# A hybrid transformer block on one core: output projection divided along its contraction, gate units moved, post norms on VectorE, exponentials ahead of the next normalisation

## What is computed

```python
def token_mixer(x, ...):        # block 1: a state space branch and an mLSTM branch
    h = rmsnorm(x, g_pre); proj = h @ w_in
    ...
    return x + rmsnorm(merged @ w_out, g_post)          # post norm 1

def channel_mixer(x, ...):
    h = rmsnorm(x, g_pre)
    a = causal_dwconv(h @ w_gate, w_conv, b_conv)
    y = (gelu(a) * (h @ w_up)) @ w_down
    return x + rmsnorm(y, g_post)                       # post norm 3

def mixer_sublayer(x, ...):     # block 2
    proj = rms_norm(x, norm_g) @ w_in                   # q, k, v, 6 forget logits, gate of 384
    q = rms_norm(q, q_gain); k = rms_norm(k, k_gain)    # per head of 64, 16 heads
    # heads 0..3 MoBA (ALiBi), 4..9 forgetting attention, 10..15 dilated attention
    y_moba = rms_norm(o_moba, out_gain[:256])
    y_fox = rms_norm(o_fox, out_gain[256:640]) * sigmoid(g_fox)
    y_dil = rms_norm(o_dil, out_gain[640:])
    return x + concatenate([y_moba, y_fox, y_dil]) @ w_out

def mlp_sublayer(x, ...):
    return x + square(relu(rms_norm(x, norm_g) @ w_up)) @ w_down
```

## Time and profile before

| | us |
|---|---|
| median of 3 timed runs | 1643.73 |
| the profiled execution's own time | 1639.23 |
| its span, first to last instruction | 1637.4 |
| TensorE busy in the span | 1510.2 |
| VectorE busy | 861.7 |
| ScalarE (ACT) busy | 669.9 |
| GpSimd (POOL) busy | 301.8 |
| mean granted TensorE clock | 0.963 |

### The profile page before, as it was taken

One profiled execution on the slowest core, in us unless ns is written; L12 is line 12 of the kernel. 1 busy time (PEld: TensorE's weight loads), 2 busy tenths in 40 slices (PEclk: granted clock), 3 DMA queues, 4 the chain that ended last, 5 costly groups with the idle time before them and its releaser, 6 DMA issues.

```text
span 1637.4 us, 22270 instructions
## 1 busy us (share of the span) xinstructions
PE 1510.2 (92%) x8565; PEld 1304.7 (80%) x8565; DVE 861.7 (53%) x1252; ACT 669.9 (41%) x1042; POOL 301.8 (18%) x280
## 2 busy tenths in 40 slices
PE   6677689999997999999998798999879999999998
PEld 6677689999996988998886576888768788888887
DVE  4877824445737453454353736677753533434344
ACT  6656685554233222222123333645462522323140
POOL 0872310000013550461262200000010000000000
PEclk9788789999998999999999899999989999999999
DMA  5111112223321333233233121111113232323331
GB/s 188 46 52 43 36 52 65 65 65 110 111 91 31 99 90 103 81 96 97 86 91 115 52 77 40 52 34 46 39 39 100 67 103 90 99 89 96 90 101 64
DMA packets 35489, 126.63 MB, mean 77 GB/s; under 512 B 4396, under 2 KB 4524, under 8 KB 35280
## 3 DMA queue, kind: packets, MB, share of 16 engines
q1 hardware_dynamic: 33888, 120.61, 24.2%
q10 hardware_dynamic: 864, 4.33, 0.7%
q0 software_dynamic: 656, 0.56, 0.1%
HBM read 123.37 MB, written 2.10 MB: 77 GB/s over the span
## 4 chain that ended last, share of the span: by engine, by line
PE 79%; DVE 10%; ACT 7%; issue 2%; POOL 2%; DMA 0%; DVEq 0%; SPq 0%; ACTq 0%; POOLq 0%
PE ps L1541 67%; PE ps L1561 2%; DVE rot L765 2%; PE ps L1840 2%; PE ps L1866 2%; ACT u L395 2%; ACT y_a L501 1%; PE ps L1690 1%; PE ps L1853 1%; ACT w_hi L324 1%; PE ps L1821 1%; DVE w_lo L762 1%; PE ps L1641 1%; POOL acc L1413 1%; POOL conv_tmp L1499 1%
## 5 line engine op out<-in xcount | busy, mean ns | idle before, releaser
L1541 PE MATMUL ps<-h_hi,w_hi 128*128 128x264 f32 (+1 forms) x1792 | 529.6, 345 | 47.0 <-DVE h_lo L774 24.8
L1541 PE MATMUL ps<-h_lo,w_hi 128*128 128x264 f32 (+1 forms) x1792 | 508.8, 333 | 0.0
L1541 PE MATMUL ps<-h_hi,w_lo 128*128 128x264 f32 (+1 forms) x1792 | 507.3, 332 | 0.0
L762 DVE TENSOR_TENSOR w_lo<-w_raw,w_hi 128x1024 fp32r<-128x1024 f32 x223 | 290.7, 1304 | 213.9 <-ACT w_hi L324 212.6
L1541 PEld LDWEIGHTS ps<-h_hi,w_hi 128*128 128x128 f32 x1792 | 310.7, 192 | 96.6 <-issue 36.0
L1541 PEld LDWEIGHTS ps<-h_lo,w_hi 128*128 128x128 f32 x1792 | 307.0, 192 | 36.4 <-issue 7.7
L1541 PEld LDWEIGHTS ps<-h_hi,w_lo 128*128 128x128 f32 x1792 | 306.6, 192 | 31.2
L324 ACT ACTIVATE w_hi<-w_raw 128x1024 fp32r<-128x1024 f32 x223 | 232.7, 1051 | 223.0 <-PE ps L1541 222.0
L1541 PE MATMUL ps<-mlp_lo,w_hi 128*128 128x512 f32 x256 | 100.9, 394 | 0.0
L1541 PE MATMUL ps<-mlp_hi,w_hi 128*128 128x512 f32 x256 | 100.4, 392 | 0.0
L1541 PE MATMUL ps<-mlp_hi,w_lo 128*128 128x512 f32 x256 | 99.4, 388 | 0.0
(11 more groups left out here) (278 smaller groups left out, 2005.7 us busy)
## 6 DMA issues: line engine op xcount, KB each, us to landing
w_raw<-w_units SPq DMA_DIRECT2D x223, 512.0 KB, 3.6
x<-x_t ACTq DMA_DIRECT2D x1, 2112.0 KB, 8.1
out<-out_tile SPq DMA_DIRECT2D x8, 256.0 KB, 2.0
x<-x_t ACTq DMA_DIRECT2D x3, 528.0 KB, 9.3
x<-x_t ACTq DMA_DIRECT2D x2, 264.0 KB, 4.6
b_raw<-ssm_b SPq DMA_DIRECT2D x1, 512.0 KB, 11.0
c_raw<-ssm_c SPq DMA_DIRECT2D x1, 512.0 KB, 12.3
dil<-dil POOLq DMA_DIRECT2D x1, 512.0 KB, 3.8
```

The costliest lines, as they stand in the source:

```text
L762: Dv.do(v.tensor_tensor(wlo[:, s % RING, :], raw[:, s % RING, :], f32(whi[:, s % RING, :]), ALU.subtract), lo_ready)
L1541: ins = mm(o, wt[:, s % RING, w], xt[:, kx, c0:c0 + n], start=(b == 0 and a == 0), stop=(b == len(blocks) - 1 and a == 2))
```

## The change

1. **Post norms.** POOL's six multiplications go; VectorE multiplies all eight tiles, each before its addition to `x`, with `h_lo` of the tile before in between.
2. **Gate units.** Gate unit 0 runs before q unit 0, gate units 1 and 2 after k unit 0. Their sigmoids run in front of iteration 1. The loop over pairs is now i = 1 .. 7.
3. **Exponentials ahead.** ACT does `exps(i-1,1)` before `qk_rsqrt(i,1)`, VectorE `weigh(i-1,1)` before `qk_norm(i,1)`. The squares of groups 0 and 1 move to iterations 5 and 6.
4. **Projection.** Its contraction is divided: eight units of five blocks (tiles 0 to 4, MoBA and gated heads; 15 matmuls each) and four units that hold the last three blocks of two output tiles each (18 matmuls). Tiles 0 to 4 are transposed, gated and split within iteration 7, into PSUM banks of the q and k units. The eight parts stand between the steps of the last three heads. The last four units write banks 2, 3, 6 and 7, from `y_dil_hi` and `y_dil_lo`. Splits of these units take 640 or 768 columns.
5. **Start of the MLP.** x, h4 and its squares follow pair by pair behind the last four units; squares have a buffer each (`mlp_sq`).

```diff
+KA, KB = 5, 3
+OB_BANK = (2, 6)
-U_QK2 = U_F2 + 1
-U_GFOX = U_QK2 + 2 * KT
-U_OUT2 = U_GFOX + 3
-U_MLP = U_OUT2 + KT
+U_G0 = U_F2 + 1
+U_QK2 = U_G0 + 1
+U_OA = U_QK2 + 2 * KT + 2
+U_OB = U_OA + KT
+U_MLP = U_OB + KT // 2
...
 ACT
+            qk_square(0, 0)
+            split_hi(qk_unit(0, 0) + LOOK)
+            qk_square(0, 1)
+            split_hi(qk_unit(0, 1) + LOOK)
+            qk_rsqrt(0, 0)
+            qk_rsqrt(0, 1)
+            split_hi(gate_unit(1) + LOOK)
+            split_hi(gate_unit(2) + LOOK)
+            for j in range(3):
+                act.wait_ge(evacuated, gate_unit(j) + 1)
+                A.do(dn.activation(sgf[:, j, :], sgf[:, j, :], ACT.Sigmoid), sem("sgf_ready"))
+            for i in range(1, KT):
+                last = i == KT - 1
+                if last:
+                    moba_gain(0)
                 if i >= 2:
                     pt_copy(i - 2, 1)
+                qk_square(i, 0)
+                if last:
+                    moba_gain(1)
+                exps(i - 1, 0)
+                split_hi(qk_unit(i, 0) + LOOK)
+                if i == KT - 3:
                     group_squares(0)
+                if i == KT - 2:
                     group_squares(1)
+                qk_rsqrt(i, 0)
+                if i == KT - 2:
                     group_rsqrt(2, 0, 2)
+                if not last:
+                    split_hi(qk_unit(i, 1) + LOOK)
+                qk_square(i, 1)
+                if last:
+                    y_hi(0)
+                    y_hi(1)
+                pt_copy(i - 1, 0)
+                if last:
+                    y_hi(2)
+                    y_hi(3)
+                    y_hi(4)
+                exps(i - 1, 1)
+                if last:
+                    split_hi(U_OA + 1)
+                qk_rsqrt(i, 1)
...
 VectorE
-                        if m < OWN_SCALED:
-                            tt(ysum[:, m, 0:n], ysum[:, m, 0:n], rs[:, 0:n], M)
-                            Dv.fence()
-                        else:
-                            dve.wait_ge(sem("y_scaled"), (KT - OWN_SCALED) * POST.index(norm) + m - OWN_SCALED + 1)
-                        stt(x[:, m, c0:T1], ysum[:, m, 0:n], col(gain, m), x[:, m, c0:T1], M, A_, sem(ready))
+                        tt(ysum[:, m, 0:n], ysum[:, m, 0:n], rs[:, 0:n], M)
                     if m:
                         dve.wait_ge(sem(hi), m)
                         stt(hlo[:, m - 1, 0:n], x[:, m - 1, c0:T1], col(pre, m - 1), f32(hhi[:, m - 1, 0:n]), M, S_, sem(lo))
+                    if m < KT:
+                        Dv.fence()
+                        stt(x[:, m, c0:T1], ysum[:, m, 0:n], col(gain, m), x[:, m, c0:T1], M, A_, sem(ready))
...
+            gate_evac(0)
+            qk_evac(0, 0)
+            split_lo(qk_unit(0, 0) + LOOK)
+            qk_evac(0, 1)
+            split_lo(qk_unit(0, 1) + LOOK)
+            qk_ms(0, 0)
+            qk_ms(0, 1)
+            qk_norm(0, 0)
+            gate_evac(1)
+            split_lo(gate_unit(1) + LOOK)
+            qk_norm(0, 1)
+            gate_evac(2)
+            split_lo(gate_unit(2) + LOOK)
+            for i in range(1, KT):
...
+                if last:
+                    y_lo(4)
+                attn_out(i - 1, 0)
+                qk_ms(i, 1)
+                if last:
+                    split_lo(U_OA + 1)
+                weigh(i - 1, 1)
+                qk_norm(i, 1)
+                if not last:
+                    split_lo(qk_unit(i, 1) + LOOK)
+            split_lo(U_OA + 2)
+            out_part(0)
+            split_lo(U_OA + 3)
+            pt_copy(KT - 2, 1)
+            out_part(1)
+            maxima(KT - 1, 0)
+            attn_out(KT - 2, 1)
+            split_lo(U_OA + 4)
+            weigh(KT - 1, 0)
+            out_part(2)
...
+            attn_out(KT - 1, 1)
+            out_part(6)
             group_ms(2, 3)
             group_norm(2, 2, 3)
...
+            out_part(7)
+            split_lo(U_OB)
+            split_lo(U_OB + 1)
+            for j in range(KB):
+                dve.wait_ge(sem("y2_hi"), KA + j + 1)
+                stt(ydlo[:, j, :], PS[:, 2 + j, :], col("out_gain", KA + j), f32(ydhi[:, j, :]), M, S_, sem("y2_lo"))
...
 POOL
-                pool.wait_ge(sem("rs_ready"), norm + 1)
-                for m in range(OWN_SCALED, KT):
-                    tt(ysum[:, m, 0:n], ysum[:, m, 0:n], rs[:, 0:n], M, sem("y_scaled"))
...
 TensorE
+            for i in range(1, KT):
+                last = i == KT - 1
+                if i >= 2:
                     pe.wait_ge(sem("qms_ready"), 2 * i - 1)
+                wide(qk_unit(i, 0))
+                if last:
+                    group_tile(0)
                 if i >= 2:
                     p_transposes(i - 2, 1)
+                if last:
+                    group_tile(1)
+                scores(i - 1, 0)
...
+            pe.wait_ge(sem("yfox_pre"), 3)
+            pe.wait_ge(sem("qms_ready"), 2 * KT - 1)
+            out_part(0)
             pe.wait_ge(sem("qms_ready"), 2 * KT)
+            out_part(1)
+            p_transposes(KT - 2, 1)
+            scores(KT - 1, 0)
+            values(KT - 2, 1)
+            out_part(2)
+            out_part(3)
+            p_transposes(KT - 1, 0)
+            scores(KT - 1, 1)
+            values(KT - 1, 0)
+            out_part(4)
+            out_part(5)
+            p_transposes(KT - 1, 1)
+            values(KT - 1, 1)
+            out_part(6)
+            out_part(7)
+            pe.wait_ge(sem("attn_done"), HEADS2)
+            pe.wait_ge(sem("dil_scaled"), 4)
+            for j in range(KB):
+                y_transposes(KA + j, 2 + j)
             pe.wait_ge(sem("y2_lo"), KT)
+            for j in range(KT // 2):
+                s = U_OB + j
+                begin(s)
+                for o in range(2):
+                    unit(s, 0, ydhi, ydlo, [(PS[:, OB_BANK[s % 2] + o, :], 0, SEQ)], None, 0,
+                         [(KB * o + k, k) for k in range(KB)], o == 1)
```

More of the change, by code:

```diff
@@ L1205, in _ @@
             ts(fz, fz, -1.0, None, M, None, sem("fox_ready"))
+            split_lo(U_G0 + LOOK)
             for j in range(2):
@@ L1301, in _ @@
                 if i >= 2:
                     attn_out(i - 2, 1)
-                if i < KT:
-                    qk_ms(i, 0)
-                split_lo(U_QK2 + 2 * i + LOOK)
-                if 1 <= i <= KT:
-                    weigh(i - 1, 0)
-                if i < KT:
-                    qk_evac(i, 1)
-                if i == KT:
-                    gate_evac(1)
+                if last:
+                    fox_gate(3)
+                qk_ms(i, 0)
+                split_lo(qk_unit(i, 0) + LOOK)
@@ L1325, in _ @@
-                if i == KT:
-                    group_norm(1, 0, 2)
-                if 1 <= i <= KT:
-                    weigh(i - 1, 1)
+                qk_evac(i, 1)
+                if last:
+                    y_lo(0)
+                    y_lo(1)
+                pt_copy(i - 1, 0)
+                if i == KT - 2:
+                    group_norm(1, 0, 2)
+                if last:
+                    fox_gate(4)
+                    y_lo(2)
+                    y_lo(3)
+                else:
+                    qk_norm(i, 0)
@@ new lines, in _ @@
+                maxima(i - 1, 1)
+                if last:
+                    y_lo(4)
+                attn_out(i - 1, 0)
+                qk_ms(i, 1)
+                if last:
+                    split_lo(U_OA + 1)
[6 more added lines that the diff above has]
+            split_lo(U_OA + 3)
+            pt_copy(KT - 2, 1)
+            out_part(1)
@@ new lines, in _ @@
+            maxima(KT - 1, 0)
[3 more added lines that the diff above has]
+            out_part(2)
+            split_lo(U_OA + 5)
+            pt_copy(KT - 1, 0)
+            out_part(3)
+            maxima(KT - 1, 1)
+            attn_out(KT - 1, 0)
+            split_lo(U_OA + 6)
+            weigh(KT - 1, 1)
+            out_part(4)
+            split_lo(U_OA + 7)
+            pt_copy(KT - 1, 1)
+            out_part(5)
+            attn_out(KT - 1, 1)
@@ new lines, in out_part @@
+            def out_part(m):
+                s = U_OA + m
+                begin(s)
+                unit(s, 0, hhi, hlo, [(PS[:, s % 2, :], 0, SEQ)], sem("y2_lo") if m == 0 else None, 0,
+                     [(k, k) for k in range(KA)])
+            wide(qk_unit(0, 0))
+            wide(qk_unit(0, 1))
+            qk_stat(0, 0)
+            qk_stat(0, 1)
+            pe.wait_ge(sem("qms_ready"), 1)
+            wide(gate_unit(1))
+            pe.wait_ge(sem("qms_ready"), 2)
+            wide(gate_unit(2))
@@ L1908, in _ @@
-            pe.wait_ge(sem("qms_ready"), 2 * KT)
-            for m in range(KT):
-                wide(U_OUT2 + m, 0, sem("y2_lo") if m == 0 else None)
-            pe.wait_ge(sem("y2_lo"), KT)
+                if last:
+                    group_tile(3)
+                qk_stat(i, 0)
+                pe.wait_ge(sem("qms_ready"), 2 * i)
```

(5 more changed lines are left out.)

235 lines of the change are left out of this document (121 added, 114 removed).

## The result

| | before | after |
|---|---|---|
| median, us | 1643.5 | 1652.0 |
| its runs | 1639.4 to 1643.8 | 1651.2 to 1653.7 |
| profiled execution (its span) | 1639.2 (1637.4) | 1653.7 (1651.9) |

The ratio is 1.0065 (95%: 1.0052 to 1.0078): the changed kernel is slower. I had forecast 1628, 1616 to 1640.

What follows compares the result with a forecast made beforehand. TensorE is busy 92% of the span, so only its waits or lower-clock time can be won. Terms -5.5-8.6+10.0-10.7+1 = -13.8 took the profiled 1639.2 to about 1625.4, given as 1628 for the median; range 1616 to 1640.

Steps and rivals of the forecast that it cites:

- post norms: Both residuals: with POOL out, VectorE's x update is quicker and TensorE starts earlier; -5.5 us, bounds -9 and 0.
- gate units in front: Before the pairs: gate units cover TensorE's waits for the q/k squares and statistics; -8.6 us, bounds -11.5 and -4.
- exponentials ahead, waits: Pair loop: k_aug comes late, TensorE waits 0.75 once and 2.1 four times; +10.0 us, bounds +1 and +16.
- the same, clock: Pair loop: no lower clock was priced behind the new k_aug waits; 0 us.
- tail, waits: Last pair to MLP's first matmul: 20.4 us idle or slow becomes 9.7 of waits; -10.7, bounds -16 and -2.
- tail, clock: Tail: the gap of 3.5 us with transposes before it may bring the lower clock; +1 us, between 0 and 1.75.
- the third term: Pair loop: the forecast's +10.0 us for the exponentials ahead of k's normalisation, one wait replaced by another.
- rival 4: Pair loop: the lower clock returns behind seven waits before scores, some 3 us each, 21 in all, 1649; chance 0.07.
- Rival 1: Pair loop: both table loads run under waits, k_aug comes in time, the loop costs 1, time 1619; chance 0.13.
- rival 3: Pair loop: a table switch costs twice its 1.28 us row, 18 us in all, time 1646; chance 0.04.
- Rival 2: Tail: late handoffs between VectorE and ACT hold up later steps, -10.7 becomes -2, time 1637; chance 0.13.

Runs made afterwards that it cites:

- four matmuls: Changed kernel with four extra matmuls (results unused) on TensorE ahead of the first scores of pairs 2 to 6; ratio 0.9942.
- the swap alone: Kernel before with only the reordering: second head's exponentials and weighing ahead of k's root and normalisation, in all seven pairs; 1659.0 us, ratio 1.0107.
- eight matmuls: Changed kernel with eight extra matmuls (results unused) on TensorE ahead of the first scores of pairs 2 to 6; ratio 0.9964.
- the best version: Changed kernel with the exponentials-ahead reordering undone in all pairs and two tail repairs (order of part 1's weight split and of y_lo); 1612.8 us, ratio 0.9833.

## Why the prediction was wrong

| step | forecast | found |
|---|---|---|
| post norms | -5.5 | -4.1 in the trace (2.3 and 1.8, from `rs` to the end of the residual), -3.4 alone on the chip |
| gate units in front | -8.6 | -8.6 |
| exponentials ahead, waits | +10.0 | +9.9 in the trace, +10.5 on the chip (+6.9 with four matmuls) |
| the same, clock | 0 | +19.6 in the trace, +16.6 on the chip (+20.2 with four matmuls) |
| tail, waits | 9.7 left | 8.2 left |
| tail, clock | +1 | +8.9 |

("In the trace" compares the stretches of two profiles, "on the chip" the ratios of timed runs. The post norms' 4.1 shrink to the 3.0 of the stretches because `rs` itself came 1.0 and 0.2 later in the profile after.)

*The step that failed* is the price of the new waits: the third term counts each as its own length and puts the clock at 0, and the tail's clock at +1. The runs show 19.6 in its place in the pairs (16.6 to 20.2 on the chip) and 8.9 in the tail. The argument for the 0 is the one by which rival 4 got a chance of 0.07: "Against it: 1145.8 to 1173.6 holds a wait of 2.51 and its mean clock is 1.00." That is one wait in one execution. In another execution of the same kernel, a wait of 2.51 of the same kind ended in scores of 1.91 and values of 4.36. I also had a hint and did not use it: two of three runs of the kernel before were 4.5 us above the profiled one. The sign that I had set for rival 4, a clock below 1.00 in the pairs, is the one that came.

Rival 4 as written, "some 3 us each, 21 in all, and the time is 1649", names the right mechanism and comes within 3 us of the 1652, but that nearness is luck: the clock fell behind fewer of the waits (in three pairs and in the tail), and each fall cost more. The three long pairs take 33.7, 33.7 and 32.1 against the 27.2 of a pair with the same wait and no fall (pair 4 of the swap alone, the pairs with eight matmuls), 6.5, 6.5 and 5 more, because the low clock lasted past the scores to the values, the statistic and the start of the next unit. Its "decides from 2 us per wait on", read as a length of wait, is no threshold: no fall behind 1.2 or 1.69 in the pairs, but one behind 1.53 at the scores of pair 6, and none behind 2.44 one pair before.

*Post norms*: the mechanism held. VectorE's x takes 0.75 with POOL silent (1.63 in the earlier trace rows), but a tile takes 2.33 and not 2.25, as two h_lo of the changed kernel show; over eight tiles that and a later finish leave 1.8 at the second norm, where I had 2.7.

```profile
903.51 0.75 DVE L835 SCALAR_TENSOR_TENSOR x<-y_sum,cols,x 128x512 f32<-128x512 f32 x1
...
905.05 0.75 DVE L835 SCALAR_TENSOR_TENSOR h_lo<-x,cols,h_hi 128x512 fp32r<-128x512 f32 x1 [0.19 <-ACT h_hi L619]
...
907.38 0.75 DVE L835 SCALAR_TENSOR_TENSOR h_lo<-x,cols,h_hi 128x512 fp32r<-128x512 f32 x1 [0.19 <-ACT h_hi L619]
```

*Gates*: no slow unit is left, and the waits are 0.64, 0.58 and 1.68 (I had 0.85 and 2.1). *Exponentials ahead*: waits of 0.83, three times 2.15, 2.44 (forecast 0.75, four times 2.1). Rival 1 (the loads hide) and rival 3 (a switch costs twice its row) are out: both loads stand in the chain above and work follows each at once. *Tail*: 3.2 for y_lo (3.5), 1.1 for ACT's copy (1.1), 1.0 for part 1's weights (1.6), 1.5 for k_aug (1.0), 0.6 for the next (1.0), 0.8 for values (1.0). Rival 2 did not happen by late handoffs. That 106.9 is 8.9 more than work and waits (89.8, the forecast's 88.9 and one statistic more, + 8.2) is the low clock: 0.92 over that stretch, against 1.00 in the best version, where the tail takes 95.9. It ran low from about 1191 to 1201.5, behind the 1.53 for k_aug, and from about 1266 to 1273, behind the 3.2 for y_lo; half of these stretches is 5.3 and 3.5. My +1 was for the second alone.

## What to carry to other kernels

Price a new wait on TensorE with the clock: in a stretch where it runs without a gap, a wait of 2.15 us before narrow matmuls cost its own length and, in five of six cases, another 5 to 6.5 for the clock. That a clock stayed up behind one wait in one profile is no evidence; profile the kernel twice more when its runs differ, and compare their mean clocks. Where such a wait can't be removed, work that nobody needs is a cheap guard (0.93 us of matmuls in a wait of 2.15 kept the clock up in the pairs), but taking the waits away was worth 7 to 10 us more.

## What the runs showed of the hardware

- The granted clock falls behind a wait of about 2 us in some places and executions and not in others: behind 2.15 and narrow masks three times of three in the changed kernel, twice of three in the kernel with the swap alone; behind 2.5 ahead of transposes once in eight such waits (three profiles of the kernel before, one of that with the norms alone); not in the pairs whose wait was 1.2 or 1.69. At the start of the tail it fell behind waits of 1.5, four times of eight, and behind 0.75 to 0.79 in the other four. What picks the one or the other is open: neither the length of the last wait, nor its place, nor the width of the work behind it decides alone, and how busy TensorE had been over a longer stretch, or where in time the wait fell, was not varied by itself.
- Once fallen, in the pairs it stayed at 1.2 GHz through scores, values, statistic and the first matmuls of the next unit, though TensorE had no further gap there; a pair then took up to 33.7 us instead of 27.2.
- Transposes of 0.11 us each held the clock up as matmuls did (0.9948 against 0.9942 and 0.9964).
